# Nine finished tiles of an encoder layer: six added onto the output by DMAs of GpSimd, three by TensorE

## What is computed

```python
    u = jnp.square(jax.nn.relu(_rms_norm(x, g_pre_ffn) @ w_up))
    x = x + _rms_norm(u @ w_down, g_post_ffn)

def _rms_norm(x, g):
    xf = x.astype(jnp.float32)
    y = xf * lax.rsqrt(jnp.mean(xf * xf, axis=-1, keepdims=True) + EPS)
    return (y * g.astype(jnp.float32)).astype(x.dtype)
```

## Time and profile before

| | |
|---|---|
| median of three executions | 2419.64 us |
| the profiled execution | 2419.09 us |
| its span, first to last instruction | 2417.3 us |
| around the span | 1.79 us |
| TensorE busy | 2391.1 us, 99% |
| VectorE busy | 1278.5 us, 53% |
| ScalarE busy | 749.5 us, 31% |
| GpSimd busy | 494.8 us, 20% |
| granted TensorE clock, mean | 0.998 |

### The profile page before, as it was taken

The page is one execution under the profiler, slowest core; times in us unless marked ns, Lnnn a source line. Parts: engine busy times, 40 slices in busy tenths (PEclk is TensorE's granted clock), DMA queues, the critical chain, the costliest instruction groups (busy, mean ns, idle before and its releaser), DMA issues.

```text
span 2417.3 us, 36774 instructions
## 1 busy us (share of the span) xinstructions
PE 2391.1 (99%) x13976; PEld 2269.4 (94%) x13976; DVE 1278.5 (53%) x2402; ACT 749.5 (31%) x1452; POOL 494.8 (20%) x729
## 2 busy tenths in 40 slices
PE   7999999999999999999999999999999999999999
PEld 7999999999999999999999999989899899898896
DVE  4153525334276667567666444544645645646638
ACT  4133232323222232322222332324233233333334
POOL 2021212111175456537545000001000000000001
PEclk9999999999999999999999999999999999999999
DMA  5252625354433323423432634223102101101104
GB/s 185 92 185 76 216 90 197 118 172 133 138 96 130 124 81 126 142 97 105 134 128 84 232 110 152 99 89 98 53 18 70 43 26 62 50 26 61 40 25 160
DMA packets 219349, 257.77 MB, mean 107 GB/s; under 512 B 8176, under 2 KB 186736, under 8 KB 219120
## 3 DMA queue, kind: packets, MB, share of 16 engines
q1 hardware_dynamic: 219248, 256.41, 31.9%
HBM read 176.16 MB, written 80.22 MB: 106 GB/s over the span
## 4 chain that ended last, share of the span: by engine, by line
PE 75%; issue 11%; DVE 8%; DMA 3%; POOL 2%; SPq 1%; ACT 1%; DVEq 0%; POOLq 0%; ACTq 0%
PE bank L619 11%; PE bank L621 11%; PE bank L620 11%; PE bank L868 6%; PE bank L870 6%; PE bank L869 6%; PE bank L918 5%; PE bank L916 5%; PE bank L917 5%; PE bank L784 1%; PE bank L897 1%; PE bank L896 1%; PE bank L898 1%; DMA ZG<-scratch_z 1%; DMA ZQ<-scratch_z 1%
## 5 line engine op out<-in xcount | busy, mean ns | idle before, releaser
L619 PE MATMUL bank<-XH,WHI 128*128 128x384 f32 x2256 | 770.1, 341 | 0.7 <-issue 0.6
L621 PE MATMUL bank<-XH,WLO 128*128 128x384 f32 x2256 | 755.4, 335 | 0.0
L620 PE MATMUL bank<-XL,WHI 128*128 128x384 f32 x2256 | 755.0, 335 | 0.0
L619 PEld LDWEIGHTS bank<-XH,WHI 128*128 128x128 f32 x2256 | 424.5, 188 | 5.0 <-issue 2.7
L620 PEld LDWEIGHTS bank<-XL,WHI 128*128 128x128 f32 x2256 | 424.5, 188 | 0.8
L621 PEld LDWEIGHTS bank<-XH,WLO 128*128 128x128 f32 x2256 | 423.9, 188 | 0.0
L1320 DVE TENSOR_TENSOR WLO<-WRAW,WHI 128x1024 fp32r<-128x1024 f32 x128 | 160.0, 1250 | 246.1 <-ACT WHI L987 241.7
L987 ACT ACTIVATE ZST<-bank 128x384 f32<-128x384 f32 x240 | 117.6, 491 | 523.4 <-PE bank L621 512.2
L868 PE MATMUL bank<-XH,WHI 128*128 128x384 f32 x768 | 256.8, 334 | 1.6 <-ACT XH L987 1.6
L870 PE MATMUL bank<-XH,WLO 128*128 128x384 f32 x768 | 256.7, 334 | 0.0
L869 PE MATMUL bank<-XL,WHI 128*128 128x384 f32 x768 | 256.6, 334 | 0.0
(11 more groups left out here) (210 smaller groups left out, 3501.1 us busy)
## 6 DMA issues: line engine op xcount, KB each, us to landing
scratch_z<-ZST SPq DMA_DIRECT2D x80, 576.0 KB, 3.1
WRAW<-in_w_in SPq DMA_DIRECT2D x80, 512.0 KB, 3.8
HZ<-scratch_z SPq DMA_DIRECT2D x32, 576.0 KB, 5.3
WRAW<-in_w_up SPq DMA_DIRECT2D x32, 512.0 KB, 4.2
WDR<-in_w_down SPq DMA_DIRECT2D x32, 512.0 KB, 5.6
MG<-scratch_z SPq DMA_DIRECT2D x16, 576.0 KB, 4.9
ZQ<-scratch_z SPq DMA_DIRECT2D x4, 1152.0 KB, 6.5
ZK<-scratch_z SPq DMA_DIRECT2D x4, 1152.0 KB, 8.5
```

The source lines that it names most:

```text
L619: pe.matmul(psum[c][:, 0:CH], WHI[p][:, k, :], XH[:, k, s], start=(k == 0), stop=False)
L620: pe.matmul(psum[c][:, 0:CH], WHI[p][:, k, :], XL[:, k, s], start=False, stop=False)
L621: last = pe.matmul(psum[c][:, 0:CH], WLO[p][:, k, :], XH[:, k, s], start=False, stop=(k == KT - 1))
```

## The change

Six of the nine tiles (j = 0, 1, 3, 5, 7, 8) lose their residual load and their addition on VectorE. Their rows of `x1` are stored, in the stage that makes `x1`, into the output tensors instead of the scratch. At the end VectorE scales these tiles in place in `ACC`, and a DMA of GpSimd with `accum_op=ALU.add` adds each onto the rows that lie in the output already. The other three (j = 2, 4, 6) stay with TensorE; j = 7 moves from TensorE to the DMAs. `OF` has three buffers instead of six, and no wait for a buffer of it is left. `X1F` is loaded for three tiles. GpSimd's loop over nine powers becomes a list written out by hand, in which six DMAs stand between the powers, each behind a wait for the scaling of its tile. SP waits for all six at the end.

```diff
-NOF = 6
+NOF = 3
-        Y_PE = (2, 4, 6, 7)
-        Y_DVE = (0, 1, 3, 5, 8)
...
+        Y_PE = (2, 4, 6)
+        Y_DMA = (0, 1, 3, 5, 7, 8)
+        T_DMA = [Y_ORDER[j] for j in Y_DMA]
...
+        def y_store(sp, i):
+            sp.wait_ge(y_pk, i + 1)
+            sp.dma_start(y_rows(Y_ORDER[Y_PE[i]]), OF[i][:, :]).then_inc(y_st, 16)
...
+            def x1_store(t):
+
+                dst = y_rows(t) if t in T_DMA else x1s[t * P:(t + 1) * P, :]
+                sp.dma_start(dst, X1R[t % 2][:, :]).then_inc(x1_st[t % 2], 16)
...
-            for j in range(NT):
+            for j in Y_PE:
                 t = Y_ORDER[j]
                 sp.dma_start(X1F[j][:, :], x1s[t * P:(t + 1) * P, :]).then_inc(x_in[j], 16)
...
-                if j >= NOF:
-                    dve.wait_ge(y_st[j % NOF], 16 * (j // NOF))
                 dve.wait_ge(gb_in, 32)
-                ch(dve.scalar_tensor_tensor(OF[j % NOF][:, :], ACC[:, t, :], yrs[:, t:t + 1], GF[:, :], ALU.mult, ALU.mult))
-                dve.wait_ge(x_in[j], 32)
-                dve.tensor_tensor(OF[j % NOF][:, :], OF[j % NOF][:, :], X1F[j][:, :], ALU.add).then_inc(y_ok, 1)
+                dve.scalar_tensor_tensor(ACC[:, t, :], ACC[:, t, :], yrs[:, t:t + 1], GF[:, :], ALU.mult, ALU.mult)\
+                   .then_inc(y_tt if j in Y_PE else y_ok, 1)
...
+            def y_onto(i):
+
+                t = Y_ORDER[Y_DMA[i]]
+                pool.wait_ge(y_ok, i + 1)
+                pool.dma_start(y_rows(t), ACC[:, t, :], accum_op=ALU.add).then_inc(y_ac, 16)
+
+            y_power(0)
+            y_onto(0)
+            y_power(1)
+            y_power(2)
+            y_power(3)
+            y_onto(1)
+            y_power(4)
+            y_power(5)
+            y_onto(2)
+            y_power(6)
+            y_power(7)
+            y_onto(3)
+            y_power(8)
+            y_onto(4)
+            y_onto(5)
```

More of the change, by code:

```diff
@@ L263, in program @@
         y_tt, y_pe, y_pk = sem("y_tt"), sem("y_pe"), sem("y_pk")
-        y_st = [sem(f"y_st{i}") for i in range(NOF)]
+        y_st, y_ac = sem("y_st"), sem("y_ac")
         zs, us, x1s = scr["z"], scr["u"], scr["x1"]
@@ L334, in program, with y_rows @@
         Y_ORDER = (4, 5, 6, 7, 0, 1, 2, 3, 8)
-        Y_PE = (2, 4, 6, 7)
-        Y_DVE = (0, 1, 3, 5, 8)
[L338 to L345, removed]
+        Y_PE = (2, 4, 6)
+        Y_DMA = (0, 1, 3, 5, 7, 8)
+        T_DMA = [Y_ORDER[j] for j in Y_DMA]
+        def y_rows(t):
+            return o["y_p"][0, t * P:(t + 1) * P, :] if t < NTP else o["y_s"].rearrange("b t d -> (b t) d")
+        def y_store(sp, i):
+            sp.wait_ge(y_pk, i + 1)
+            sp.dma_start(y_rows(Y_ORDER[Y_PE[i]]), OF[i][:, :]).then_inc(y_st, 16)
         def ret_mixed(e):
@@ L557, in _ @@
                     sp.wait_ge(d_x1, t)
-                    sp.dma_start(x1s[(t - 1) * P:t * P, :], X1R[(t - 1) % 2][:, :]).then_inc(x1_st[(t - 1) % 2], 16)
+                    x1_store(t - 1)
             sp.wait_ge(d_x1, NT)
-            sp.dma_start(x1s[(NT - 1) * P:, :], X1R[(NT - 1) % 2][:, :]).then_inc(x1_st[(NT - 1) % 2], 16)
+            x1_store(NT - 1)
             def up_w(g, b):
@@ L582, in _ @@
             sp.dma_start(GF[:, :], a["g_post_ffn"].to_broadcast([P, D])).then_inc(gb_in, 16)
-            for j in range(NT):
+            for j in Y_PE:
                 t = Y_ORDER[j]
                 sp.dma_start(X1F[j][:, :], x1s[t * P:(t + 1) * P, :]).then_inc(x_in[j], 16)
-            for j in range(NT):
-                y_store(sp, j)
             for i in range(NOF):
-                sp.wait_ge(y_st[i], 16 * ((NT + NOF - 1 - i) // NOF))
+                y_store(sp, i)
+            sp.wait_ge(y_st, 16 * NOF)
+            sp.wait_ge(y_ac, 16 * len(Y_DMA))
             sp.wait_ge(H.sr_st, 16 * HH + 16)
@@ L973, in _ @@
             y_x1(0)
-            for i in range(4):
-                if i < 3:
+            for i in range(NOF):
+                if i < NOF - 1:
                     y_x1(i + 1)
@@ L1302, in _ @@
             for i, j in enumerate(Y_PE):
-                if j >= NOF:
-                    act.wait_ge(y_st[j % NOF], 16 * (j // NOF))
                 for q in range(2):
                     act.wait_ge(y_pe, 2 * i + q + 1)
-                    last = copy(OF[j % NOF][:, 512 * q:512 * (q + 1)], psum[2 * i + q][:, :])
+                    last = copy(OF[i][:, 512 * q:512 * (q + 1)], psum[2 * i + q][:, :])
                 last.then_inc(y_pk, 1)
@@ L1923, in _, with y_power @@
             pool.memset(ACC[:, :, :], 0.0).then_inc(acc0, 1)
-            for j in range(NT):
+            def y_power(j):
                 t = Y_ORDER[j]
```

## The result

The changed kernel took 2423.51 us (median of 22 executions, 2422.02 to 2424.27) against 2419.55 for the kernel before (22 executions on the same chips): 4.0 us more. The ratio is 1.0016, 95% interval 1.0011 to 1.0022. It is slower, and the interval leaves out 1, by less than the 0.2% that the prediction took as the bound. Forecast was a gain of 1.2 us, to 2418.4, with a range of 2415.0 to 2423.5.

What follows compares the result with a forecast made beforehand. The queue on the DMA engines, not TensorE, was to set the end: from 2406.9, three adding tiles at 1.94 and two stores at 1.29, then 0.8, 0.5 and 1.79, give 2418.4 us; 8-in-10 range 2415.0 to 2423.5.

Steps and rivals of the forecast that it cites:

- m: Time one adding tile of 512 KB holds the DMA engines; taken as 1.94 us, midway between one transfer and two.
- rival 1: On the DMA engines, an adding tile's two operands pass one after the other, 2.59 us a tile: 2420.5 us; chance 0.26.
- The start of the queue: On the DMA engines in the last stage: from 2406.9 three adding DMAs and two stores wait in turn, 8.4 us.
- The landing after the last byte: At the end of the span: 0.8 us from the end of moving to landing, read from the last two stores before.
- Ahead of the stage: nothing: Before the last stage: moved stores of x1 and six fewer loads into X1F are hidden and worth nothing now.
- TensorE's part: Last stage: without tile j = 7, 3.44 us go and three tiles end at 2408.6.
- VectorE's part: Last stage: five residual additions of 1.23 us go; seven scalings of 1.26 would end at 2408.0 without any wait.
- GpSimd's part: Last stage: six DMAs between the powers make scalings 6 and 8 wait; the last DMA is out at 2410.0.
- c: Time a DMA takes on GpSimd; bounded by 0.33 and 1.52 us, taken as 1.0.
- Rival 2: On the DMA engines, cheap adding DMAs, 1.29 us a tile and 0.33 on GpSimd: 2415.5 us; chance 0.16.
- Rival 3: GpSimd becomes the bound, each DMA taking 3 us on it: 2421.0 us; chance 0.12.
- Rival 4: The addition is serial in each DMA engine, 4.3 us a tile: 2427.3 us, slower; chance 0.10.

Runs made afterwards that it cites:

- e1: The changed kernel with 2048 instead of 1024 bytes of each partition for the descriptors of GpSimd's DMAs; 2422.89 us, ratio 1.0015 to the kernel before.
- e3: The changed kernel with GpSimd's fourth adding DMA moved behind the power of the last tile; 2423.53 us, ratio 1.0015 to the kernel before.
- e5: The changed kernel with 3072 bytes for descriptors and three more adding DMAs of 512 KB behind GpSimd's sixth; 2431.16 us.
- e4: The changed kernel with adding DMAs for j = 5, 7, 8 alone, and the residual of j = 0, 1, 3 on VectorE; 2422.97 us.
- e2: The changed kernel with accum_op taken out of GpSimd's six DMAs, which store without adding; 2416.62 us, ratio 0.9988 to the kernel before.
- e6: The changed kernel with 3072 bytes for descriptors and three more adding DMAs of 256 KB (512 columns) behind GpSimd's sixth; 2427.64 us.
- e7: The changed kernel with 3072 bytes for descriptors and three more plain DMAs of 512 KB behind GpSimd's sixth; 2426.41 us.

## Why the prediction was wrong

**The mechanism was right, the sizes were not, and with them the direction.** That six tiles would no longer be bound by TensorE but by the queue of adding DMAs and stores on the DMA engines is what the trace shows: between 2407 and 2415 their share is 0.97 (the sign against it was a share under 0.9), and the last thing to land is an adding DMA. e1 and e3 confirm it: what GpSimd and VectorE gain or lose in between moves the end by 0.6 at most. But the queue costs more than TensorE's fourth tile did. The end of the span is 2421.2 against 2416.6 in the sum, 4.6 later. In the terms of that sum:

- *m, the time of an adding tile*: taken 1.94, "midway between one transfer and two", because "a part of the read may pass beside the write". e5 measures 2.5 (2.76 by the medians). Three such tiles stood in the queue at the end: 3 x 0.57 = 1.7 us. This is the step that failed most. The bound of two transfers stood in the text, with a rule behind it, and was priced as rival 1; no row spoke for anything less. The Trainium skill's rule of two reads for a reducing transfer (Collectives: The Full Stack, "The bandwidth ceiling: the fold count and why AG ≠ RS ≠ AR") agrees with the trace: 2.48 us against 1.28 is 1.9 times a plain DMA, and 2 by the page.
- *The start of the queue*: 2406.9 in the sum; in the trace it is 2408.5 (share 0.15 in the half microsecond before, 0.98 after), 1.6 later. The fourth DMA was given at 2407.70 instead of 2405.9. The hold behind it was in no term; among the waits on GpSimd I had counted those written in the code only. Taken away alone (e1), it gives back 0.3 to 0.6, since the engines are then busy with the third adding tile and a store. The sum had that tile through at 2405.1, and it landed at 2407.5, so most of this term too is what an adding tile costs.
- *The slow start of a burst of adding DMAs*: in no term. From 2408.5 bytes move until about 2419.9 (90 GB/s in the half microsecond from 2419.5, 8 in the next), 11.4 us for three adding tiles and two stores, which at 2.5 and 1.29 are 10.1: 1.3 more. In 2410.0 to 2411.5 the engines write 82 GB/s instead of 211, which alone loses 0.9 us. The lone adding tiles start so too (28, 73, 124, then 192 in the GB/s row). Why stays open, and so does the other 0.4.
- *The landing after the last byte*: 0.8 taken, and 0.8 from about 2419.9 to 2420.7. It held.

The first three add up to 4.6. The cost of a tile and the hold are measured by runs of their own (e5, e1); the slow start is read from the traces only. As a sign for m the text had the last tile landing some 6 us after it is given; it was 9.9.

**Ahead of the stage: nothing** held: the last product starts 0.06 from where it was. In the stretch of the loads of x1 the engines move 202 GB/s instead of 405, which is worth nothing, as said.

**TensorE's part** held: 3.44 us go, the end is at 2408.8 against 2408.6.

**VectorE's part** held: the last gather starts at 2398.51 (2398.5), the scalings follow at 1.26, and the first DMA at the front is hidden: scaling 1 starts at 2395.03 (2395.05).

**GpSimd's part** held but for the hold. c was taken as 1.0. Its rows show 0.86 to 1.03 and once 1.23, and what follows starts 0.5 to 0.8 after the DMA does, so as an obstacle it is nearer 0.7. It does run under scalings of VectorE (e1: 2404.70, e4: 2405.92), once with 1.40. The Trainium skill's warning that such a DMA starves while VectorE holds the shared ports (SBUF — State Buffer, "SBUF: two separate sides"), which it tells of VectorE's 2-port modes, doesn't show with scalings that read two tiles; its narrower sentence in "Who interferes with whom", by which a two-input operation takes only the read side, agrees.

**The rivals.** Rival 1 (m = 2.59, 2420.5) had the right m to within 0.1 and missed the hold and the slow start. Rival 2 is out: adding costs (e2). Rival 3 expected GpSimd's last DMA after 2411 for a slow giving; it was given at 2410.82, but for lack of room, and wasn't the bound. Rival 4's serial addition would have given 12.9 us in e5; it was 8.3 by the medians, 7.5 in the traces.

**The range** ended at 2423.5 and the median is 2423.51. Above it lay rival 4 and a quarter of rival 3; nothing stood there for an m of two transfers together with another loss. Terms that err in the same direction should be added at their upper ends once: an m of two transfers (2.59) gives 3 x 0.65 = 2.0, and with the 1.6 and the 1.3 above it is 2418.4 + 4.9 = 2423.3.

## What to carry to other kernels

Here an adding DMA of 512 KB cost the DMA engines twice a store and landed 3 us later than one (5.5 against 2.6), so it pays where its landing is hidden, not as the last thing of a kernel. Moving work off the engine that bounds the end is worth only what the next queue leaves, and that queue has to be added up in transfers, each at its own cost, with the moment from which it never empties. A wait that the profile puts down to an engine long done, on an engine that gives DMAs itself, is worth comparing with the landings of its earlier ones.

## What the runs showed of the hardware

- With 1024 bytes set aside (`dynamic_dma_scratch_size`), the fourth adding DMA of 128 rows waited until the third had landed (2407.5 and 2407.70; in e3 2407.8 and 2408.05). The first two had landed before, by 2402.5. With 2048 it didn't wait, and with plain DMAs (e2) six went through in 1024.
- An adding DMA of 512 KB holds the engines for 2.5 us in a full queue (e5: 2.51 in the traces, 2.76 by the medians; 211 GB/s written), one of 256 KB for 1.6 (e6), a plain one of 512 KB for 1.2 to 1.3 (e7; 410 GB/s).
- A burst of adding DMAs starts slowly: 82 GB/s in its first 1.5 us in the changed kernel, 211 later, with the engines' share at 1.0 in both.
- Powers of one column on GpSimd wait for VectorE's scalings (2.77 for a pair instead of 1.1), its DMAs hardly do (0.88 under a scaling at 2402.08, 1.03 without one at 2392.55).
